# The 31-tap depthwise convolution of a conformer layer moved from VectorE to TensorE

## What is computed

```
def dwconv(x, w):
    k = w.shape[0]
    return lax.conv_general_dilated(
        x, w[:, None, :].astype(x.dtype), window_strides=(1,),
        padding=[((k - 1) // 2, k // 2)],
        dimension_numbers=("NWC", "WIO", "NWC"),
        feature_group_count=x.shape[-1])

def conformer_conv(h, w1, b1, dw, dwb, ln_g, ln_b, w2, b2):
    u = h @ w1 + b1
    a, g = jnp.split(u, 2, axis=-1)
    u = a * jax.nn.sigmoid(g)
    u = dwconv(u, dw) + dwb
    u = jax.nn.silu(layernorm(u, ln_g, ln_b))
    return u @ w2 + b2
```

## Time and profile before

| | us |
|---|---|
| median of 3 runs | 3190.74 (3190.43 to 3191.28) |
| the profiled execution | 3191.89 |
| its span | 3190.1 |
| PE busy in the span | 2964.5 |
| DVE busy | 1723.3 |
| ACT busy | 1258.3 |
| POOL busy | 354.1 |

### The profile page before, as it was taken

The page is one execution under the profiler, slowest core; times in us unless marked ns, Lnnn a source line. Parts: engine busy times, 40 slices in busy tenths (PEclk is TensorE's granted clock), DMA queues, the critical chain, the costliest instruction groups (busy, mean ns, idle before and its releaser), DMA issues.

```text
span 3190.1 us, 41428 instructions
## 1 busy us (share of the span) xinstructions
PE 2964.5 (93%) x17444; PEld 2490.3 (78%) x17444; DVE 1723.3 (54%) x2618; ACT 1258.3 (39%) x2032; POOL 354.1 (11%) x372
## 2 busy tenths in 40 slices
PE   8998999989999989999975399999999999998898
PEld 7997898879977757888752178887887888787898
DVE  6664554655545545444599854443545444444565
ACT  5443443654444434222344343232324322334443
POOL 0000000000013210000178100000000000143100
PEclk9999999999999999999997699999999999999999
DMA  6545666656655443232446132322323233266354
GB/s 228 185 161 187 227 229 219 194 199 226 215 145 87 75 126 119 92 105 93 140 160 241 40 119 94 104 93 94 118 93 118 94 95 103 69 127 92 110 185 133
DMA packets 344459, 441.34 MB, mean 138 GB/s; under 512 B 9777, under 2 KB 329297, under 8 KB 331985
## 3 DMA queue, kind: packets, MB, share of 16 engines
q1 hardware_dynamic: 339744, 428.66, 40.6%
q0 software_dynamic: 4368, 9.45, 4.5%
q10 hardware_dynamic: 160, 0.59, 0.1%
HBM read 437.61 MB, written 1.05 MB: 138 GB/s over the span
## 4 chain that ended last, share of the span: by engine, by line
PE 79%; DVE 13%; ACT 4%; DMA 2%; issue 1%; POOL 0%; SPq 0%; DVEq 0%; ACTq 0%
PE ps L1074 23%; PE ps L1076 23%; PE ps L1075 23%; DVE CV L1876 5%; DVE lo L1566 2%; DVE lo L1569 1%; PE ps L1095 1%; PE ps L1097 1%; PE ps L1096 1%; PE ps L1246 1%; PE ps L1116 1%; ACT hi L1276 1%; PE ps L1107 1%; PE ps L1234 1%; PE ps L1155 1%
## 5 line engine op out<-in xcount | busy, mean ns | idle before, releaser
L1074 PE MATMUL ps<-XN,hi 128*128 128x256 f32 (+1 forms) x3008 | 1020.8, 339 | 78.5 <-DVE lo L1566 37.4
L1075 PE MATMUL ps<-XN,hi 128*128 128x256 f32 (+1 forms) x3008 | 1004.2, 334 | 0.0
L1076 PE MATMUL ps<-XN,lo 128*128 128x256 f32 (+1 forms) x3008 | 1003.8, 334 | 0.0
L1074 PEld LDWEIGHTS ps<-XN,hi 128*128 128x128 f32 x3008 | 580.1, 193 | 189.9 <-issue 36.1
L1566 DVE TENSOR_TENSOR lo<-raw,hi 128x1024 fp32r<-128x1024 f32 (+1 forms) x313 | 390.0, 1246 | 449.9 <-ACT hi L1276 425.4
L1076 PEld LDWEIGHTS ps<-XN,lo 128*128 128x128 f32 x3008 | 579.7, 193 | 54.3
L1075 PEld LDWEIGHTS ps<-XN,hi 128*128 128x128 f32 x3008 | 580.2, 193 | 51.6
L1276 ACT ACTIVATE hi<-raw 128x1024 fp32r<-128x1024 f32 (+1 forms) x313 | 326.4, 1043 | 501.0 <-PE ps L1076 430.5
L1569 DVE TENSOR_TENSOR lo<-raw,hi 128x1024 fp32r<-128x1024 f32 (+1 forms) x313 | 385.1, 1230 | 0.0
L1076 PE MATMUL ps<-H,lo 128*128 128x512 f32 (+1 forms) x1024 | 371.2, 363 | 0.0
L1074 PE MATMUL ps<-H,hi 128*128 128x512 f32 (+1 forms) x1024 | 371.2, 363 | 0.0
(11 more groups left out here) (228 smaller groups left out, 3535.9 us busy)
## 6 DMA issues: line engine op xcount, KB each, us to landing
raw<-in_mlp_w SPq DMA_DIRECT2D x128, 1024.0 KB, 5.2
raw<-in_mod_w SPq DMA_DIRECT2D x96, 1024.0 KB, 5.0
raw<-in_ffn_w_in SPq DMA_DIRECT2D x44, 1024.0 KB, 5.8
raw<-in_attn_w_in SPq DMA_DIRECT2D x36, 1024.0 KB, 5.6
raw<-in_na_wqkv SPq DMA_DIRECT2D x24, 1024.0 KB, 5.2
raw<-in_ffn_w_out SPq DMA_DIRECT2D x16, 1024.0 KB, 5.1
raw<-in_mlstm_w_in SPq DMA_DIRECT2D x12, 1024.0 KB, 5.4
raw<-in_cv_w SPq DMA_DIRECT2D x12, 1024.0 KB, 5.6
```

The costliest lines, as they stand in the source:

```text
L1074: e.matmul(out, whi, xhi, start=first, stop=False)
L1075: e.matmul(out, whi, xlo, start=False, stop=False)
L1076: i = e.matmul(out, wlo, xhi, start=False, stop=last)
```

## The change

- The gate half of the input projection is now made before the value half. DVE takes the value half straight from PSUM, adds its bias and multiplies by the sigmoid in one instruction (`cv_a`), into one of four buffers of `U`.
- For each tile `k`, SP copies `U` inside SBUF with 16 DMAs (`cv_spread`): for each of the four groups `g` of 32 features and each shift `i` of 0 to 3, 32 partitions of 572 columns, shifted by `i`, to the 32 partitions `32 i` of `UX[.., g, ..]`. So the 128 partitions of one `UX` row hold 32 features at four consecutive shifts. `UX` has three buffers.
- DVE builds the weights of a tile, `WD`: for each group and each `j` of 0 to 7 a 128x32 matrix with the tap `4 j + i` of a feature on the diagonal of block `i` (one multiplication of 128x1024 elements, from the new inputs `taps` and `group`).
- PE convolves: for `j` of 0 to 7 and `g` of 0 to 3 a float32 matmul of the 128x32 weights with 512 columns of `UX` starting at `4 j`, all summed in one bank, group `g` on partitions `32 g` (`cv_conv`). ACT evicts the bank with the bias into `CV`.
- Tiles 2c-2 and 2c-1 are convolved behind the gate unit of round `c`, tiles 6 and 7 behind the last unit, each behind one modulation unit.
- The totals over features: DVE adds tiles 0 to 6 in `SA` (`cv_total`), PE does one matmul with ones on that sum and one on tile 7.
- The loop up to modulation unit 45 and the interleaving of taps are gone. One modulation unit stands between the mean and the centring, one behind `rstd`. Modulation units stand in the conformer layer from number 29 to 41 (before: to 45) and in the MLP behind it from 41 to 46 (before: 45 to 46), at a pace of 0.125.

The core of the diff:

```diff
-    p.apart.append(convolve_apart((1, 3, 5)))
+
+    def convolve(k):
+        p.do("cv_conv", k, *p.bank())
+        p.do("cv_total", k, p.use(6)[1] if k == KT - 2 else p.bank_use[6])
+        p.flush()
+
     p.pace = 1.0
     for c in range(4):
+        def evac_g(t, b, u):
+            p.do("cv_g", c, t, b, u)
+
         def evac_a(t, b, u):
-            p.do("cv_a", c, t, b, u)
-
-        def evac_g(t, b, u):
-            k = 2 * c + t
-            p.do("cv_g", c, t, b, u)
-            u_made.add(k)
-            if c < 3 and t == 0:
-                p.background.append(convolve((k,)))
-            elif c == 3 and t == 1:
-                p.background.append(convolve((k - 1, k)))
-
-        p.linear("cv_w1_2", 0, 0, KT, c * 256, 256, x, evac_a, adv=7, outer=c == 0)
-        p.linear("cv_w1_2", 0, 0, KT, 1024 + c * 256, 256, x, evac_g, adv=7)
+            p.do("cv_a", 2 * c + t, t, b, u)
+            p.do("cv_spread", 2 * c + t)
+
+        p.linear("cv_w1_2", 0, 0, KT, 1024 + c * 256, 256, x, evac_g, outer=c == 0)
+        for k in (2 * c - 2, 2 * c - 1):
+            if k >= 0:
+                convolve(k)
+        p.linear("cv_w1_2", 0, 0, KT, c * 256, 256, x, evac_a)
     p.pace = p.credit = 0.0
-    while p.mods < 45:
+    for k in (KT - 2, KT - 1):
         p.mod_unit()
-        p.advance(8)
         p.flush()
-    totals(4)
-    p.folds()
-    while p.apart:
-        p.advance()
-    p.drain()
-    totals(KT)
+        convolve(k)
+    p.sa_user = "cv_summed"
     p.do("tables", LNEXP)
     p.do("cv_mean", p.bank_use[6], p.rs_user)
+    p.mod_unit()
+    p.flush(True)
```

```diff
+    def cv_spread(k):
+        w.wait_ge(("cv_u", k), ("conv", k - 3) if k >= 3 else None)
+        for g in range(4):
+            for i in range(4):
+                e.dma_start(m.UX[32 * i:32 * i + 32, k % 3, g, 0:572],
+                            m.U[32 * g:32 * g + 32, k % 4, i:i + 572]).then_inc(
+                    *sig[f"ux{k % 3}"].says(("ux", k)))
...
+    def cv_conv(k, b, u):
+        w.wait_ge(("ux", k), ("wd", k), free_of(b, u))
+        for j in range(8):
+            for g in range(4):
+                rows = m.UX[:, k % 3, g, :].rearrange("p (s t) -> p s t", s=2)
+                f = e.matmul(m.ps[b][32 * g:32 * g + 32, :], m.WD[:, k % 2, g, j, :], rows[:, :, 4 * j:4 * j + S],
+                             start=j == 0, stop=j == 7)
+        f.then_inc(*acc.says(("acc", b, u), ("conv", k)))
...
+    def cv_a(k, t, b, u):
+        w.wait_ge(("acc", b, u), ("cv_s", k), "cv_pads", ("ux", k - 4) if k >= 4 else None)
+        e.scalar_tensor_tensor(
+            out=m.U[:, k % 4, :].rearrange("p (s t) -> p s t", s=2)[:, :, 15:271],
+            in0=m.ps[b].rearrange("p (s t) -> p s t", s=2), scalar=param(m, "cv_b1_2", k),
+            in1=m.SGM[:, k // 2 % 2, t, :].rearrange("p (s t) -> p s t", s=2), op0=ALU.add, op1=ALU.mult).then_inc(
+            *dve.says(("free", b, u), ("cv_u", k)))
+        w.wait_ge("taps", "consts", ("conv", k - 2) if k >= 2 else None)
+        e.tensor_tensor(m.WD[:, k % 2, :, :, :].rearrange("p g j c -> p (g j) c"),
+                        m.taps[:, k, :, :].rearrange("p g j -> p (g j)").unsqueeze(2).broadcast_to([P, 32, 32]),
+                        const(m, "group").unsqueeze(1).broadcast_to([P, 32, 32]), ALU.mult).then_inc(
+            *dve.says(("wd", k)))
+
+    def cv_total(k, u):
+        if 0 < k < KT - 1:
+            w.wait_ge(("cv_sum", k), ("cv_add", k - 1) if k > 1 else None)
+            e.tensor_tensor(m.SA[:, :], m.CV[:, 0, :] if k == 1 else m.SA[:, :], m.CV[:, k, :], ALU.add).then_inc(
+                *dve.says(("cv_add", k)))
 
```

More of the change, by code:

```diff
@@ L79, in constants @@
     put("sign", np.repeat([-1.0, 1.0], 16)[:, None])
+    put("group", np.tile(np.eye(32), (4, 1)))
     put("freq", np.array(ROPE_FREQ + ROPE_FREQ, np.float32)[:, None])
@@ L147, in allocate @@
     m.sem = {n: ctx.enter_context(nc.semaphore(f"s_{n}"))
[L148 removed]
+             for n in ["acc", "act", "high", "dve", "low", "pool", "ld", "x0", "x1", "taps", "ux0", "ux1", "ux2", "pv", "ci", "pos", "cst", "tb0", "tb1", "out"]
              + [f"raw{i}" for i in range(RAW)]}
@@ L328, in flush @@
             f()
-        if fold and not self.apart:
+        if fold:
             self.folds()
@@ L784, in conformer @@
     p.do("cv_pads", s)
[L785 to L817, removed]
@@ L1248, in na_mix @@
         f.then_inc(*acc.says(("acc", b, u), ("na_mixed", layer, i), ("na_group", layer, group)))
-    def cv_total(k, at, u, apart):
-        w.wait_ge(("cv_sum", k), free_of(6, u) if at == 0 else None)
-        f = e.matmul(m.ps[6][:, 0:512], ones, m.CV[:, k, :], start=at == 0, stop=at == KT - 1)
-        if at == KT - 1:
-            f.then_inc(*acc.says(("acc", 6, u)))
+    def cv_conv(k, b, u):
[7 more added lines that the diff above has]
+    def cv_total(k, u):
+        if k == KT - 2:
+            w.wait_ge(("cv_add", k), free_of(6, u))
+            e.matmul(m.ps[6][:, 0:512], ones, m.SA[:, :], start=True, stop=False).then_inc(*acc.says("cv_summed"))
+        if k == KT - 1:
+            w.wait_ge(("cv_sum", k))
+            e.matmul(m.ps[6][:, 0:512], ones, m.CV[:, k, :], start=False, stop=True).then_inc(
+                *acc.says(("acc", 6, u)))
     w.wait_ge("consts")
@@ L1991, in cv_pads @@
         w.wait_ge(("xn", s, KT - 1))
-        for a in (0, 271):
-            e.memset(m.U[:, :, :, a:a + 15], 0.0).then_inc(*pool.says("cv_pads"))
-    def cv_tap_apart(k, i, before):
-        if i:
-            out = m.CV[:, k, :]
-            w.wait_ge(("cv_mul", k, i), ("cv_apart", k, i - 1))
-            e.tensor_tensor(out, out, m.TAP[:, i % 4, :], ALU.add).then_inc(
-                *pool.says(("cv_apart", k, i), ("cv_sum", k) if i == 30 else None))
+        for a, b in ((0, 15), (271, 288)):
+            e.memset(m.U.rearrange("p b (s t) -> p (b s) t", s=2)[:, :, a:b], 0.0).then_inc(*pool.says("cv_pads"))
     def sc_pads(s):
```

78 lines of the change are left out of this document (29 added, 49 removed), and 2 rows, old and new, of the table ROWS.

## The result

| us | before | the changed kernel |
|---|---|---|
| median | 3190.59 (3188.25 to 3191.28, 4 runs) | 3213.99 (3211.20 to 3216.17, 4 runs) |
| ratio to before | | 1.0074 [1.0057, 1.0092] |
| the profiled execution, its span | 3191.9, 3190.1 | 3211.2, 3209.0 |
| first product of the stage | 1565.06 | 1561.37 |
| the stage, to the first product of the output projection | 260.0 | 275.4 |

The change makes the kernel slower, by 0.74% or 23.4 us. I had forecast 9.7 us faster. The time lies inside the range of 8 in 10, on the side of the rival "the copies are slow".

The account below looks back on a forecast made before the run. DVE's taps were taken to bound the conformer stage, PE the rest. Stage: 147.2 + 44.1 + 25.3 + 23.6 = 240.2 against 260.0 us, -19.8; with costs outside net -9.9, giving 3181 us, 8-in-10 range 3170 to 3228.

Parts of the forecast that it names:

- the copies are slow: Rival, SP's queue: 32 row copies issue or move slowly before each blocked load; 3205 at 0.6, 3227 at 0.78 us; chance 0.30.
- What bounds the kernel, and what the change removes: Conformer stage, 260.0 us: DVE's taps bound it, PE elsewhere; the change takes all taps off DVE.
- The convolution on PE: PE in the conformer stage: 64 matmul records a tile take 6.9 us, eight tiles 55 us.
- dear convolution: Rival, PE's convolution: each record pays its weight load, 7 us more a tile, 3237; or groups run serially; chance 0.07.
- the case in which the four groups do not run together: Part of a rival, PE's convolution: column groups run one after the other, some 165 us more; shared chance 0.07.
- The wait for the load: PE idles 13.1 us for a modulation load behind SP's copies; 14.7 with lower clock, 44.1 in three rounds.
- 32 copies at 0.41 us: SP's queue: issuing the row copies ahead of the modulation load takes 13.1 us, each copy between 0.37 and 0.78.
- the sensitivity given: Forecast time: one hundredth of a microsecond per copy is worth 1.26 us, 3 x 0.32 plus 0.3 in the fourth round.
- N - 4.45: When SP starts the copies, counted from when the unit whose output they wait for leaves PE (N).
- The tail: Last total to output projection's first product: 17.3 us before, +3.5 for pair and fold, +2.8 for weight split: 23.6.
- Landing and bandwidth: DMA in the stage: load lands some 5.3 us after issue; a copy's data takes 0.20 to 0.78 us.
- Outside the stage: Next MLP: four moved modulation units cost 2.1 us each, 8.5, and a fold 1.1; tap load at start at most 0.3.

## Why the prediction was wrong, point by point

**What bounds the kernel, and what the change removes.** Right. All taps left DVE, and what took their place was a wait elsewhere.

**The convolution on PE.** Right: two tiles, 128 records, run in 13.9 us, 6.9 a tile, as taken from the earlier trace rows. The rule of the Trainium skill's "TensorE: Matmul & The Clock Gate", part 3, that weight loads overlap only where the row group differs, does not hold for these four column groups, which share their rows: 512 loads of 0.11 us would have added 56 us. Rival "dear convolution" is out, and with it the case in which the four groups do not run together.

**The wait for the load: the step that failed.** The place of the waits, how many there are and what releases them were right. The failed term is "32 copies at 0.41 us": it was 0.63. For the choice I leaned on the small size of the copy and on lone loads; but every row has its source in HBM, and none a copy inside SBUF; the source is what turned out to matter (0.46 against 0.63 in a row of issues). Of the 22 hundredths some 5 lie in the row of issues itself, which cost 0.46 from HBM too, and 17 in the source. By the sensitivity given, 22 hundredths are 27.7 us, 21.1 in the three rounds and 6.6 in the fourth: 3208.7. The rest up to 3214, by the first profile's stage (275.4 against 240.2 + 27.7 = 267.9), is 7.5 us:
- In the first round SP began at N - 2.0 and not at N - 4.45, because a split stood ahead of DVE's gate (the later SP start that I had named as the price if DVE's cover failed): 2.4.
- In the fourth round PE came out of its wait at a lower clock, which I had charged to three rounds only. The convolution of tile 6 took 9.80 us instead of 7.05, tile 7 0.6 more, a modulation product 0.9 more: about 4.
- The lower clock behind the other three waits: from one N to the next, less the idle and the work at the prices of my sum, it cost 2.3, 2.1 and 1.3 us against 1.5 each: 1.2 in all. (A fold took about 0.45 us and not my 1.12, so behind the first and the third wait the clock cost 0.7 more than that, and the folds as much less.)
- The tail was 23.9 against 23.6, though its two terms were 1.1 too large: so the remainder of my tail was too short by 1.4.

These come to about 8; the idles of the second and third round were 0.2 us each shorter than the sum gives at 0.63.

Of the clock, the stretches of the changed kernel show the lower of its two levels (0.50, that is 1.2 of 2.4 GHz) behind the first wait and in the first 4.65 us of tile 6, and most of the full one right after (0.91):

```profile
1610.50:1614.50 4.00, 3.92 (x13) 1.87 (x14) 0.00 (x0) 1.58 (x3) 0.00 (x0) 0.50 1.09 401
1785.35:1790.00 4.65, 4.65 (x24) 1.18 (x28) 0.00 (x0) 0.00 (x0) 0.00 (x0) 0.50 0.48 117
1790.00:1795.00 5.00, 5.00 (x44) 1.16 (x36) 0.00 (x0) 0.00 (x0) 0.00 (x0) 0.91 0.48 117
```

**Landing and bandwidth.** Right: the load feeds PE 5.3 us after its issue, and a copy lands in 2.0 us, under others. The Trainium skill's rule on small transfers ("DMA: Bandwidth & Descriptors", "Rules for kernel authors": coalesce, since under 64 KB one pays mostly overhead) was good advice, for a reason other than the one I weighed it by: a copy of 73 KB lies just above that size, and what fewer transfers saved was issues. The 2 us were paid side by side, as I said; the issues were paid one after the other.

**Outside the stage.** Forecast +9.6 behind it, measured +7.2 and +8.9.

**The chances.** The rival "slow copies" had the mechanism and the sign, with its turning point at 0.49 us and 3209 at the measured price. I gave it 0.30 and the forecast 0.50. pos, the only row of 32 partitions, said 0.74, and gb with 8 said 0.58; I set both aside as odd. They may have had other reasons, since their source is HBM, but they were all that spoke of unusual forms. With bounds of 0.37 and 0.78 and a turning point at 0.49, most of the span between the bounds lay on the slower side.

## What to carry to other kernels

Count the DMAs, not only their bytes: each is an instruction on an in-order queue, and 32 of them, three times over, in front of a load that PE needs cost more than the stage gained by having 178 us less to do on DVE. If a change puts a burst of issues on a queue, ask for every load behind it when it is needed, and bring those forward first; here that one edit turned 0.7% slower into 1.5% faster. Where the price of an operation is missing from the trace, and the bounds lie on both sides of the point at which the change turns, say so by the chances, and let the middle of the bounds decide, not the hoped-for end.

## What the runs showed that I had not expected

- A DMA from SBUF to SBUF keeps its issuing engine 0.59 us at the median (0.62 to 0.71 from start to start, single issues up to 2.11), whether it moves 8, 73 or 293 KB and over 32, 64 or 128 partitions. From HBM it is 0.33 alone and 0.43 in a row of loads (0.46 from start to start), the same with 32 and 128 partitions. A store to HBM took 0.33 alone, and 0.43 directly behind four loads. On ACT the copies cost 0.68 from start to start. I have no cause for the difference by source, only the numbers.
- A store of 288 KB issued behind four loads of 286 KB landed in 4.6 to 6 us instead of 2.1.
- A wait costs something beside itself: the 64 matmul records of tile 6 took 7.05 us behind no wait, 8.56, 8.77 and 8.68 behind waits of 3.10, 2.99 and 5.88 us, and 9.49 to 9.98 behind waits of 5.98 to 12.43. The length of the wait alone does not settle it (8.68 behind 5.88, 9.98 behind 5.98).
